# Decoder trunk on Trainium2: ScalarE instead of VectorE scales the low part of a differential pair's output

## The reference

```python
def _diff_attention(q, k, v, lam, lam_init, norm_g):      # 4 heads, two maps m each
    ...
        s = jnp.einsum('bqhmd,bkhmd->bhmqk', q_blk, k) * scale
        s = s - slopes[None, :, None, None, None] * dist[None, None, None]
        s = jnp.where(dist >= 0, s, NEG_INF)
        p = jax.nn.softmax(s, axis=-1)
        a = (p[:, :, 0] - lam * p[:, :, 1]).astype(v.dtype)
        return jnp.einsum('bhqk,bkhe->bqhe', a, v)
```

## Time and profile before

| | us |
|---|---|
| median of 3 runs | 2052.26 |
| lowest and highest | 2048.38, 2054.08 |
| the profiled execution's own time | 2058.27 |
| its span in the trace | 2056.5 |
| TensorE busy | 1950.1 (95%) |
| VectorE busy | 1112.6 (54%) |
| ScalarE busy | 703.3 (34%) |

### The profile page before, as it was taken

How to read it: one execution, slowest core, us unless ns; L and a number is a source line. 1 busy time by engine, 2 the same in 40 slices (tenths; PEclk the granted TensorE clock), 3 DMA queues, 4 the chain that set the end, 5 groups by cost and what they waited for, 6 DMA issues and landing times.

```text
span 2056.5 us, 25255 instructions
## 1 busy us (share of the span) xinstructions
PE 1950.1 (95%) x9341; PEld 1632.3 (79%) x9341; DVE 1112.6 (54%) x1792; ACT 703.3 (34%) x1017; POOL 327.9 (16%) x291
## 2 busy tenths in 40 slices
PE   7999999997989999999999999999978899999996
PEld 6888888886777888888788888888867788888885
DVE  6444445562776653444584444546647765444446
ACT  4323322343434433333242222224335343233321
POOL 6000000333314400000150000003332252000002
PEclk9999999998979999999999999999989999999998
DMA  5223233226731323222322223231277132322221
GB/s 219 102 82 107 78 120 110 80 85 176 190 88 62 116 71 119 102 82 102 113 97 88 102 82 120 74 132 70 78 204 193 42 108 78 121 98 86 102 102 41
DMA packets 41922, 216.99 MB, mean 106 GB/s; under 512 B 8724, under 2 KB 9172, under 8 KB 17928
## 3 DMA queue, kind: packets, MB, share of 16 engines
q1 hardware_dynamic: 38984, 200.35, 27.9%
q0 software_dynamic: 2880, 15.90, 3.1%
HBM read 198.28 MB, written 17.93 MB: 105 GB/s over the span
## 4 chain that ended last, share of the span: by engine, by line
PE 80%; DVE 10%; issue 3%; DMA 2%; ACT 2%; SPq 2%; POOL 1%; DVEq 0%; ACTq 0%; POOLq 0%
PE bank L857 74%; PE bank L1020 2%; SPq L391 2%; DVE res L1283 1%; DVE nat L1431 1%; DMA whiD<-stacks 1%; DMA rawA<-in_a_w 1%; PE bank L1116 1%; PE bank L885 1%; DVE st L1307 1%; DVE hl L1358 1%; DVE hl L1542 1%; DVE wlam L1532 1%; PE bank L1104 1%; DVE negm L1515 1%
## 5 line engine op out<-in xcount | busy, mean ns | idle before, releaser
L857 PE MATMUL bank<-whiD,hl 128*128 128x512 f32 x1408 | 444.6, 390 | 5.6 <-DVE hl L1358 5.1
L1283 DVE SCALAR_TENSOR_TENSOR res<-bank,res 128x512 f32<-128x512 f32 x384 | 258.5, 688 | 171.0 <-PE bank L857 168.8
L857 PEld LDWEIGHTS bank<-whiD,hl 128*128 128x128 f32 x1408 | 264.3, 188 | 65.0 <-DVE hl L1358 8.1
L857 PE MATMUL bank<-xhi,whiA 128*128 128x512 f32 (+1 forms) x768 | 287.6, 374 | 10.3 <-DVE xlo L1262 10.3
L857 PE MATMUL bank<-xlo,whiA 128*128 128x512 f32 (+1 forms) x768 | 285.9, 372 | 0.0
L857 PE MATMUL bank<-xhi,wloA 128*128 128x512 f32 (+1 forms) x768 | 285.9, 372 | 0.0
L857 PE MATMUL bank<-wloD,hl 128*128 128x512 f32 x704 | 274.1, 389 | 0.0
L857 PE MATMUL bank<-xhi,whiB 128*128 128x512 f32 x704 | 273.9, 389 | 0.0
L857 PE MATMUL bank<-xlo,whiB 128*128 128x512 f32 x704 | 273.9, 389 | 0.0
L857 PE MATMUL bank<-xhi,wloB 128*128 128x512 f32 x704 | 273.9, 389 | 0.0
L857 PEld LDWEIGHTS bank<-xhi,whiA 128*128 128x128 f32 x768 | 145.5, 189 | 38.0 <-DVE xlo L1262 8.5
(11 more groups left out here) (177 smaller groups left out, 3146.8 us busy)
## 6 DMA issues: line engine op xcount, KB each, us to landing
rawA<-in_a_w SPq DMA_DIRECT2D x63, 1024.0 KB, 4.8
rawB<-in_b_w SPq DMA_DIRECT2D x54, 1024.0 KB, 4.8
rawD<-in_d_w SPq DMA_DIRECT2D x46, 1024.0 KB, 4.8
stacks<-hl SPq DMA_DIRECT2D x240, 64.0 KB, 1.7
whiD<-stacks POOLq DMA_DIRECT2D x10, 768.0 KB, 6.0
wloD<-stacks POOLq DMA_DIRECT2D x10, 768.0 KB, 6.0
gbr<-in_gb_row SPq DMA_DIRECT2D x7, 1024.0 KB, 6.4
out<-nat SPq DMA_DIRECT2D x4, 512.0 KB, 2.6
```

The source lines that it names most:

```text
L857: ins = t_.matmul(out_, a_, b_, start=(start and k == 1), stop=(stop and k == n), skip_group_check=check)
L1283: v.scalar_tensor_tensor(out=r, in0=bank[b][:, :], scalar=scale, in1=r, op0=ALU.mult, op1=ALU.add).then_inc(step, 1)
```

## The change

In the two differential bodies VectorE no longer scales the low part of the output. ScalarE does, with a `Copy` activation that has the reciprocal as its scale, and it does so in its own list behind the exponentials of the step and ahead of `p_hi`. VectorE's second operation (`scalar_tensor_tensor`) stays where it was and waits for `olo_ok`, which now comes from ScalarE. FoX bodies are as before. In each layer 16 operations move, 32 in all.

```diff
--- before.py
+++ after.py
@@ -777,6 +777,13 @@
                         a.activation(s32[:, i, 0:w], bank[i][:, 0:w], ACT.Exp, bias=negm[:, i:i + 1],
                                      accum_out=rsum[:, i:i + 1]).then_inc(exp_ok[m], 1)
 
+                def low_part(G):
+
+                    act.wait_ge(pv_done, l * ALL + G + 1 + AHEAD)
+                    act.wait_ge(rinv_ok, l * ALL + G + 1)
+                    a.activation(olo[:, G % 2, :], bank[4 + G % 2][:, HD:2 * HD], ACT.Copy,
+                                 scale=rinv[:, G % STEPS, 0:1]).then_inc(olo_ok, 1)
+
                 def p_hi(G):
                     w = (G % NT + 1) * P
                     act.wait_ge(pt_done, l * ALL + G + 1)
@@ -814,6 +821,8 @@
                 for G in range(ALL):
                     b, k = divmod(G, STEPS)
                     exp(G)
+                    if G >= 2 and is_diff(G - 2):
+                        low_part(G - 2)
                     if G:
                         p_hi(G - 1)
                     if k == 0 and b + 1 < BODIES:
@@ -1550,7 +1559,8 @@
                     o = nat[:, t, c:c + HD]
                     dve.wait_ge(rinv_ok, l * ALL + G + 1)
                     b_ = bank[4 + G % 2]
-                    v.tensor_scalar(olo[:, G % 2, :], b_[:, HD:2 * HD], rinv[:, j, 0:1], None, ALU.mult).then_inc(olo_ok, 1)
+                    if not is_diff(G):
+                        v.tensor_scalar(olo[:, G % 2, :], b_[:, HD:2 * HD], rinv[:, j, 0:1], None, ALU.mult).then_inc(olo_ok, 1)
                     dve.wait_ge(olo_ok, l * ALL + G + 1)
                     v.scalar_tensor_tensor(out=o, in0=b_[:, 0:HD], scalar=rinv[:, j, 0:1], in1=olo[:, G % 2, :],
                                            op0=ALU.mult, op1=ALU.add).then_inc(o_ok, 1)
```

## The result

| | before | after |
|---|---|---|
| median | 2053.17 us (6 runs) | 2062.47 us (6 runs) |
| lowest and highest | 2048.38, 2055.87 | 2060.84, 2062.96 |
| the profiled execution's own time | 2058.27 | 2060.84 |

The change makes the kernel slower by 0.45%, 95% interval 0.33% to 0.57%: 9.3 us, between 6.8 and 11.7. The forecast was 0.19%. The two profiled executions are only 2.6 us apart, because that of before lies 5 us above its median and that of after is the fastest of its six; so I compare steps, not spans.

The account below looks back on a forecast made before the run. In the heads the chain through VectorE was taken to set the pace. 12 covered steps x 0.32 = 3.84 us, all other terms at nothing, gave a forecast median of 2056.1 us (0.19% more), range 2051.0 to 2062.5.

Parts of the forecast that it names:

- A: Main case: only the covered steps in the heads pay, as summed; 2056.1 us, bounds 2054.5 to 2060, chance 0.62.
- B: Rival: longer TensorE waits in body 1 make its clock fall; 2061 us in one layer, 2066 in both; chance 0.22.
- signs of being wrong: Lower granted clock in bodies 1 and 2; ScalarE's operation or handing over much longer; `p_hi` after a differential body delaying TensorE.
- C: Rival: something unseen, such as a transfer the heads wait for, takes up the added time; 2052.3 us, chance 0.11.
- D: Rival: VectorE is the true bound, its freed time comes through in late steps; 2.2 us less, 2050.1, chance 0.05.
- The 12 named steps: Body 1 steps 2, 3, 6, 7 and body 3 steps 6, 7, both layers: each 0.32 us longer, 3.84 us.
- GpSimd's cover: Body 1 step 5 and body 3 step 3: a shorter GpSimd wait absorbs the delay; nothing, or 1.3 us if gone.
- The late step 4 of body 1 and step 2 of body 3: `values` ends after the exponentials, scaling already on the path: nothing; -0.7 to +0.6 us over all eight late steps.
- the two steps behind body 1: Steps without a mix after a differential body: TensorE waits cover the low part; 0, or 1.2 us if cover went.
- the 0.32 us of a step: Covered differential step: mix starts 0.41 us after the exponentials instead of 0.09, so the step is 0.32 longer.
- the hand-over from ScalarE to VectorE: From the end of ScalarE's low part to VectorE's start of the output: 0.02 us.
- The upper bound of the step: Covered step at most 0.48 us longer, with a 0.38 us `Copy` and the mix waiting for the output's full 0.28.

Follow-up runs that it names:

- spare: Kernel before plus a 64 wide scaled copy on ScalarE in all 32 steps, constant tile into a tile nobody reads; VectorE still scales: 1.0005 against before.
- place: Kernel before, VectorE still scaling the low part, but first waiting for the step's exponentials in the 32 steps: 1.0044 against before.
- twice: Changed kernel with a second scaled copy of the same 64 columns on ScalarE ahead of the real one, into an unread tile: 1.0063 against before.
- mixfirst: Changed kernel with VectorE's mix ahead of the output in differential steps: 1.0021 against before.
- moved_after: Changed kernel with GpSimd's two operations on gbr moved from body 3 to body 0: 2054.25 us, 1.0004 against before.
- body1: Kernel before with the change made in differential body 1 only: 1.0022 against before.
- first: Changed kernel with ScalarE's low part ahead of the step's exponentials instead of behind them: 1.0039 against before.
- noscale: Changed kernel with ScalarE copying the low part without multiplying it by the reciprocal: 1.0026 against before.
- body3: Kernel before with the change made in differential body 3 only: 1.0007 against before.
- moved_before: Kernel before with GpSimd's two operations on gbr moved from body 3 to body 0: 2042.74 us, 0.9941 against before.
- warm_after: Changed kernel with matmuls nobody reads added where TensorE waits in body 1 and in step 0 of body 2: 1.0034 against before.

## Why the prediction was right, and where its size was off

**How close it was.** The range ended at 2062.5 and the median is 2062.47: that it was held is in part luck (with three more runs the median of before had risen by 0.9 us besides). The loss of 9.3 us is 2.4 times the forecast 3.84, the result lies above A's own upper bound of 2060, and the chance given to less than 0.3% was 0.69. So the right account is A with a part of B, and of the signs of being wrong that the prediction lists two came: the granted clock is lower in body 1, and the handing over takes longer. C and D fall, since the interval begins at 6.8 us.

**The mechanism was right.** The heads are paced through VectorE, the scaling had lain beside the exponentials, and the change puts it behind them. Taking VectorE out of it (spare), leaving ScalarE out (place), doubling the piece (twice) and putting the mix ahead (mixfirst) agree on that.

**Which steps pay: right.** The 12 named steps do. GpSimd's cover held in step 5 of body 1 where the clock held, and in step 3 of body 3 (7.71 to 7.77, 7.47 to 7.47; the mix's scalar operation went from 3.46 to 2.65 us in layer 0), until moved_after took it away. The late step 4 of body 1 and step 2 of body 3 cost nothing, as said: with the clock held, steps 4 and 5 of body 1 together stay as they were. In the trace of after the two steps behind body 1 stayed at 3.36 and 2.00 us. TensorE's waits grew from 11.7 to 14.1 us in layer 0 and from 12.2 to 13.2 in layer 1; about 2 in each were forecast, from 11.

**The term that was mis-sized: the 0.32 us of a step.** It measured 0.43. The low part took 0.31 for 0.30. The rest is the hand-over from ScalarE to VectorE, forecast at 0.02 and measured at 0.13, because I had taken it from `p_lo` behind `p_hi`. The upper bound of the step, 0.48, held. Twelve steps make 5.1 us and not 3.8.

**The term that was kept out of the sum: rival B.** I gave the clock's fall 0.22 and put its price at up to 5 us for a layer. Over 38 us from body 1's start in layer 0 the granted clock is 0.96 in the changed kernel, body1, first, mixfirst, noscale, twice and moved_after, in all of which the steps of body 1 are longer; in layer 1 it is 0.91 in the changed kernel, 0.96 in four of the others and 1.00 in first and mixfirst. It is 1.00 in both layers of the kernel before, spare, body3 and moved_before, which keep the old steps, and of warm_after, where TensorE's waits are filled. It is not a rival to A but comes on top, since the change itself lengthens the waits behind which it came.

Two parts of B were off. Its price in a layer is 0.67 and 1.27 us in the changed kernel's trace, 1.6 us where the fall comes in body 2, as B had it, and 3.8 us in layer 0 of moved_after, where the clock fell twice in body 2. And the length of a wait doesn't decide by itself, so no point between 1.12 and 1.52 us does: in body1 the clock held through 1.42 in one layer and fell behind 1.42 in the other, and in twice it held through 1.64 in layer 0.

**What stays open.** 5.1 and 1.9 make 7.0 of 9.3 us, inside the interval. The other 2.3 aren't found in a trace. They may be time at the lower clock, which differs from one execution to the next: in body 2, as above, or in body 3, where over 45 us from its start layer 0 had 0.70 in the profiled execution of before and 0.81 in that of after. No run here settles it, nor what decides whether the clock falls behind a given wait.

The Trainium skill's rule in "ScalarE: Activation LUTs", "Rules for kernel authors", that a multiplication belongs on VectorE, came out right here, but not by the operation's own time: that differs by 0.03 us (0.28 on VectorE, 0.31 on ScalarE), and it is the place that cost.

## What to carry to other kernels

Moving an operation to a less busy engine takes it off nothing if it lay beside a wait; look at what its new place in the other engine's list is behind. Here ScalarE's list put a 0.3 us piece behind the very instructions that the next link of the chain waits for, and each 0.1 us between them was paid in full (0.10 less a step in noscale, 0.20 more in twice). Before trading microseconds between engines, look for long operations on the chain that are long because another engine holds them: moving 3.8 us of GpSimd's work in each layer took 12.1 us off the kernel, where this change added 9.3.

## What the runs showed of the hardware

- VectorE started 0.13 us after the end of ScalarE's 64 column operation, with and without the scale, but 0.02 after the end of the 512 column one, and 0.10 after the exponentials' sum in mixfirst. The runs don't say what makes the difference.
- A second `Copy` of 64 columns directly behind the first costs 0.19 us, though they are listed with 0.31 and 0.32.
- With the same waits in body 1 (0.9 and 1.42 us), the granted clock fell behind the 1.42 in both layers of the changed kernel and in layer 1 of body1, and held in layer 0 of body1. In the kernel before, with waits of up to 1.12 there, it held in both. Useless matmuls in such waits can be worth their time: 21 of them in each layer took 4.3 us off the kernel before.
- GpSimd's operations hold VectorE's L1532, whose inputs all lie in SBUF, to their end: 3.46 us for a 0.22 us operation. It took 0.22 when GpSimd's work was moved. With the change, VectorE came to it later and it took 2.65.
